# Turning the next quarter of x behind the product blocks of two tiles, in place of at the quarter's change

## The reference, cut to what matters

```
h = rmsnorm(x, norm_w)                       # x is 2048 x 1024
u = h @ w_in                                 # here the columns of RWKV
mixed = u + (prev_token(u) - u) * mu         # r, k, v and the two low-rank inputs
decay = exp(-exp(w(tanh(wl)))), a = sigmoid(al @ a_up + a0)
S_t = S_{t-1} (diag(w_t) - kk_t^T (a_t kk_t)) + v_t^T k_t ;  y_t = S_t r_t
out = (groupnorm(y) + bonus) * silu(g)
```

## Time and profile before

| | |
|---|---|
| median of 3 runs | 3938.05 us (3936.14 to 3941.47) |
| the profiled execution's own time | 3943.03 us |
| its span, first to last instruction | 3941.3 us |
| PE busy in the span | 3507.1 us (89%) |
| DVE, ACT, POOL busy | 1894.0, 1273.3, 798.4 us |
| stream stage, from the span's start to its last instruction | 1066 us |

### The profile page before, as it was taken

How to read it: one execution, slowest core, us unless ns; L and a number is a source line. 1 busy time by engine, 2 the same in 40 slices (tenths; PEclk the granted TensorE clock), 3 DMA queues, 4 the chain that set the end, 5 groups by cost and what they waited for, 6 DMA issues and landing times. The chain is left out here.

```text
span 3941.3 us, 72212 instructions
## 1 busy us (share of the span) xinstructions
PE 3507.1 (89%) x30237; PEld 2860.4 (73%) x30237; DVE 1894.0 (48%) x2915; ACT 1273.3 (32%) x1970; POOL 798.4 (20%) x592
## 2 busy tenths in 40 slices
PE   6989989899698898797999998960699999999998
PEld 4777878778534344586888886850699999999997
DVE  4455656556522133366212225669455555555553
ACT  3343534444221222233000002330344444444442
POOL 3333434333167093000000000011010010110100
PEclk9999999999899899898999999985899999999999
DMA  4121121111132131343110105440466666666663
GB/s 129 45 79 45 43 82 43 55 47 29 60 121 79 44 107 33 128 136 94 27 53 27 53 11 183 155 138 13 158 199 218 203 214 204 201 218 207 208 207 86
DMA packets 357752, 431.44 MB, mean 109 GB/s; under 512 B 14788, under 2 KB 301684, under 8 KB 356004
## 3 DMA queue, kind: packets, MB, share of 16 engines
q1 hardware_dynamic: 348328, 394.82, 31.1%
q0 software_dynamic: 9216, 33.56, 3.6%
HBM read 361.04 MB, written 67.13 MB: 109 GB/s over the span
## 5 line engine op out<-in xcount | busy, mean ns | idle before, releaser
L1983 PE MATMUL bank<-ex_x_hi,ex_w_lo 128*128 128x256 f32 x2048 | 580.3, 283 | 1.5 <-DVE ex_x_lo L2152 1.5
L1984 PE MATMUL bank<-ex_x_lo,ex_w_hi 128*128 128x256 f32 x2048 | 580.2, 283 | 0.0
L1985 PE MATMUL bank<-ex_x_hi,ex_w_hi 128*128 128x256 f32 x2048 | 580.1, 283 | 0.0
L1979 DVE TENSOR_TENSOR ex_w_lo<-ex_w_loaded,ex_w_hi 128x2048 fp32r<-128x2048 f32 x186 | 420.7, 2290 | 235.6 <-ACT ex_w_hi L1975 235.6
L1975 ACT ACTIVATE ex_w_hi<-ex_w_loaded 128x2048 fp32r<-128x2048 f32 x192 | 359.8, 1905 | 199.6 <-PE bank L1985 183.9
L1983 PEld LDWEIGHTS bank<-ex_x_hi,ex_w_lo 128*128 128x128 f32 x2048 | 393.9, 192 | 2.5 <-issue 1.9
L1984 PEld LDWEIGHTS bank<-ex_x_lo,ex_w_hi 128*128 128x128 f32 x2048 | 393.8, 192 | 0.6
L1985 PEld LDWEIGHTS bank<-ex_x_hi,ex_w_hi 128*128 128x128 f32 x2048 | 393.8, 192 | 0.0
L1227 PE MATMUL bank<-hidden_hT,gl_w_block 128*128 128x512 f32 x768 | 335.1, 599 | 1.4 <-ACT gl_ada_acc L1341 1.4
L1778 PE MATMUL bank<-sc_x_hi,sc_w_lo 128*128 128x512 f32 x768 | 300.4, 391 | 21.8 <-DVE sc_hT_lo L1814 16.3
L1779 PE MATMUL bank<-sc_hT_lo,sc_w_hi 128*128 128x512 f32 x768 | 299.5, 390 | 0.0
(11 more groups left out here) (334 smaller groups left out, 7083.6 us busy)
## 6 DMA issues: line engine op xcount, KB each, us to landing
ex_w_loaded<-in_wg SPq DMA_DIRECT2D x64, 1024.0 KB, 5.2
ex_w_loaded<-in_wu SPq DMA_DIRECT2D x64, 1024.0 KB, 6.5
ex_w_loaded<-in_wd SPq DMA_DIRECT2D x64, 1024.0 KB, 5.2
rw_w_loaded<-in_w_in SPq DMA_DIRECT2D x68, 512.0 KB, 3.9
gl_ada_tile<-in_ada_w SPq DMA_DIRECT2D x48, 512.0 KB, 3.9
sc_w_loaded<-in_sc_w_in SPq DMA_DIRECT2D x24, 512.0 KB, 6.9
rw_x_tile<-in_x SPq DMA_DIRECT2D x16, 512.0 KB, 4.9
hT_dram<-rw_h_staged SPq DMA_DIRECT2D x32, 256.0 KB, 2.8
```

The costliest lines, as they stand in the source:

```text
L1979: engine.tensor_tensor(w_lo[c % SPLIT][:], raw[:, c % LOADED, :], w_hi[c % SPLIT][:].bitcast(F32), ALU.subtract).then_inc(s["lo"], 1)
L1983: nc.tensor.matmul(psum, ll, rh, start=first, stop=False)
L1984: nc.tensor.matmul(psum, lh, rl, start=False, stop=False)
L1985: return nc.tensor.matmul(psum, lh, rh, start=False, stop=last)
```

## The change

The staging buffer is gone. A result of turning is written back into the half of the x tile that it was read from (`staged`), and rounding, subtraction and the store read it there. Turning goes by halves of four transposes, numbered x = 0 to 7 in a quarter, one ring job each. In the last two tiles of a quarter (i % 4 is 2 or 3) one half is turned after the PE work of parts 2 and 4 of the first half and of parts 1 and 3 of the second (`turned_in`), and DVE and SP take it one part later (`staged_in`). The rounding and subtraction of all eight stand at the quarter's change: those of the first four blocks of rows at the end of the last tile, the others in part 0 of the next one (`split_in`). The product k of that tile waits for the two portions apart. The first tile of a quarter then has its jobs in the order k, lr, w, a, r, v, g, with r, v and g in halves as in other tiles. Loading, squares and scaling of x are in the first and second tile of the quarter instead of the last. Before the first tile all eight halves are turned and split at once.

```
+        staged = lambda x: xt[:, x // 2 % 4, x % 2 * 512:x % 2 * 512 + 512].rearrange("p (k t) -> p k t", t=P)
...
-                return ({4: ("k",)}, {0: ("lr",), 1: ("r",), 3: ("v",), 4: ("g",)})[half].get(part, ())
+                return ({1: ("k",), 2: ("lr",)}, {0: ("r",), 2: ("v",), 4: ("g",)})[half].get(part, ())
...
+        def turned_in(i, half, part):
+
+            n = {(0, 2): 0, (0, 4): 1, (1, 1): 2, (1, 3): 3}.get((half, part))
+            if n is None or i >= NT - HP or i % HP < 2:
+                return ()
+            return (8 * (i // HP + 1) + 4 * (i % HP - 2) + n,)
+
+        def staged_in(i, half, part):
+
+            return turned_in(i, half, part - 1) if part else turned_in(i - 1 + half, 1 - half, 4)
+
+        def split_in(i, half, part):
+
+            if (half, part) == (1, 4) and i < NT - HP and i % HP == HP - 1:
+                return [8 * (i // HP + 1) + 2 * n for n in range(4)]
+            if (half, part) == (0, 0) and HP <= i < NT and i % HP == 0:
+                return [8 * (i // HP) + 2 * n + 1 for n in range(4)]
+            return []
...
                     for part in parts:
+                        if name == "k" and i % HP == 0:
+                            pe.wait_ge(s["h_lo_p"], 4 * q + 2 * part + 2)
+                            pe.wait_ge(s["h_lo_v"], 4 * q + 2 * part + 2)
...
+                    if i < NT and half == 0 and i % HP == 0:
+                        if part < 2:
+                            product(i, ("k", "lr")[part], (0, 1))
+                        elif part == 2:
                             decay_and_a(i)
+                        else:
+                            product(i, "r", (part - 3,))
...
+                    for x in turned_in(i, half, part):
+                        turn_x(x)
                     if half == 1 and part == 4:
                         if i < NT:
                             bonus_sum(i)
                         if 0 <= i - 3 < NT:
                             turn_y(i - 3)
-                        if i % HP == HP - 1 and i < NT - 1:
-                            turn_x(4 * (i // HP + 1))
...
+                def load_x(q):
+
+                    sp.wait_ge(s["h_lo_p"], 4 * q)
+                    sp.wait_ge(s["h_lo_v"], 4 * q)
+                    for n in range(4):
+                        sp.wait_ge(hs_out[n], 32 * q)
+                        sp.dma_start(xt[:, n, :], x[0, (4 * q + n) * P:(4 * q + n + 1) * P, :]).then_inc(x_in[n], 16)
...
+                        for e in staged_in(i, half, part):
+                            keep_h(e)
+                        if half == 0 and part == 1 and i % HP == 0 and i < NT - HP:
+                            load_x(i // HP + 1)
                         for name in finished(i, half, part):
...
                     if i < NT and i % HP == 0:
+                        if (half, part) == (0, 2):
+                            keep_lora(i // HP)
+                            keys(i)
+                        if (half, part) == (0, 3):
+                            decay_and_a(i)
                         if (half, part) == (1, 0):
                             exponents(i)
...
-                    if i % HP == HP - 1 and i < NT - 1:
+                    if i % HP == 1 and i < NT - HP:
                         q = i // HP + 1
```

More of the change, by code:

```diff
@@ L442, in _ @@
                 pe.wait_ge(s["small"], 16 * SMALL)
-                turn_x(0)
+                for x in range(8):
+                    turn_x(x)
                 for g in slots:
@@ L535, in _ @@
                     load(n)
+                for e in range(8):
+                    keep_h(e)
                 load(3)
@@ L539, in _ @@
                     for part in range(5):
[L540 to L545, removed]
+                        if half == 0 and part == 0 and 0 <= i - 4 < NT:
+                            store(i - 4)
+                        for e in staged_in(i, half, part):
+                            keep_h(e)
+                        if half == 0 and part == 1 and i % HP == 0 and i < NT - HP:
+                            load_x(i // HP + 1)
                         for name in finished(i, half, part):
@@ L548, in _ @@
                             load(n + 4)
-                        if half == 0 and part == 1 and 0 <= i - 4 < NT:
-                            store(i - 4)
                 sp.wait_ge(s["stored"], 16 * NT)
                 for n in range(4):
-                    sp.wait_ge(hs_out[n], 16 * 8)
+                    sp.wait_ge(hs_out[n], 32 * Q)
             @block.scalar
@@ L660, in pump @@
                 def pump(i, half, part):
-                    for t in x_of(i, half, part):
-                        keep_hi(2 * t)
-                        keep_hi(2 * t + 1)
+                    for e in split_in(i, half, part) if half == 0 else []:
+                        keep_hi(e)
                     for name in finished(i, half, part):
@@ L726, in _ @@
                     split_hi(n)
+                for e in (0, 2, 4, 6, 1, 3, 5, 7):
+                    keep_hi(e)
                 act.wait_ge(s["derived"], 1)
@@ L935, in pump @@
                             mix_raw(i, "r", r)
+                    if i < NT:
                         if (half, part) == (1, 1):
@@ L944, in pump @@
                             form_of_r(i)
-                    if i % HP == HP - 1 and i < NT - 1 and (half, part) == (1, 0):
+                    for e in staged_in(i, half, part):
+                        keep_h(e)
+                    for e in split_in(i, half, part)[1::2] if half else []:
+                        keep_lo(e)
+                    if i % HP == 1 and i < NT - HP and (half, part) == (1, 0):
                         scale_x(i // HP + 1)
@@ L1016, in _ @@
                     nc.vector.tensor_scalar(xt[:, t, :], xt[:, t, :], xst[:, 3, t:t + 1], None, ALU.mult).then_inc(s["scaled"], 1)
+                for e in range(8):
+                    keep_h(e)
+                for e in (2, 6, 3, 7):
+                    keep_lo(e)
                 for g in slots:
@@ L1103, in _ @@
                     split_lo(n)
+                for e in (0, 4, 1, 5):
+                    keep_lo(e)
                 for g in slots:
@@ L1111, in _ @@
                     for part in range(5):
-                        for t in x_of(i, half, part):
-                            keep_lo(2 * t)
-                        if i < NT and (half, part) == ((1, 2) if i % HP == 0 else (0, 2)):
+                        for e in split_in(i, half, part)[0::2] if half == 0 else []:
+                            keep_lo(e)
+                        if i < NT and (half, part) == ((0, 4) if i % HP == 0 else (0, 2)):
                             before_step(i)
@@ L1121, in _ @@
                             split_lo(windex[(i, name)] + 3)
+                        for e in split_in(i, half, part)[0::2] if half else []:
+                            keep_lo(e)
         meet(nc, s)
```

148 lines of the change are left out of this document (55 added, 93 removed).

## The result

The changed kernel takes 3990.99 us in the median of 4 runs (3989.33 to 3993.06), where the kernel before took 3937.1 beside it (3934.55 to 3941.47). The ratio is 1.0136 [1.0121, 1.0151]: 54 us slower. The direction was the one forecast, the size was not: 3959 was named, with 3980 as the upper end.

The account below looks back on a forecast made before the run. PE was taken to bound the stream stage. Terms -48.3 + 64.7 + 3.0 - 1 + 3 made +21 us on the profiled 3943.03, 3964, less 5.0 to the median: 3959 us, range 3934 to 3980.

Parts of the forecast that it names:

- gain at the three quarter changes: Stretches around each quarter's change, without half turnings, take 96.6 us each instead of 338.1 in all: 48.3 us gained, bounds 36 and 64.
- turnings in six tiles: Tiles 2, 3, 6, 7, 10, 11 each get 2.2 us of PE transposes of x: 13.2 us cost.
- ring waits: With x between jobs, blocks wait for later readers in the two-bank ring: 8.8 us a tile, 51.5 in six, bounds 40 and 62.
- scaling: Scaling x, now in a quarter's second tile, stands before a copy of the next slot: 1.0 us three times, bounds 0 and 4.
- start: At the start k could begin 3.6 us earlier, but the low-rank chain stands open: -1 us, bounds -4 and +5.
- clock: PE's clock falls after waits of 3.6 us at two of six places: 3 us, bounds 0 and 22.
- wait 1.9: At a quarter's change, block k waits 1.9 us for its first portion of low parts.
- wait 2.3: At a quarter's change, block k waits 2.3 us for the second portion, behind ACT and DVE's and POOL's subtractions.
- I take 1.8: At a quarter's change, w waits 1.8 us, between 0 and 3.5, for the low-rank inputs.
- New wait 3.6, 2.6, 1.6, 1.0: Per turning tile: r waits for k's mix, v for r's, g for v's, bonus for ACT's reading of g, in that order.
- The clock falls at every longer ring wait: Rival, chance 0.13: 11 waits of 2.6 and 3.6 us each followed by 12 matmuls at 1.2 GHz, +17 over forecast, 3976 us.
- wait for weights: Rival, chance 0.09: x loads ahead of g's weights delay ACT up to 8 us at tiles 0, 4, 8; 3975 to 3983.

Follow-up runs that it names:

- experiment 1: The changed kernel, but the block after a turned half takes that half's bank and DVE reads the half at once: 3910.05 us, ratio 0.9936 to the kernel before.
- experiment 3: The kernel before, turning unchanged, with the change's waits of r, v, g and bonus added in tiles 2, 3, 6, 7, 10, 11: 4008.73 us, ratio 1.0178.
- experiment 6: The kernel before with only block g's wait for the mix of v added in the six tiles: 3948.17 us, ratio 1.0025.
- experiments 7 and 8: Experiment 1's kernel plus the change's waits by hand, 3987.82 us (7); or plus 16, 11 and 7 extra matmuls ahead of r, v, g, 3965.45 us (8).
- its repeat: Experiment 1's kernel measured once more, unchanged: 3914.36 us, ratio 0.9942 to the kernel before.
- experiments 4 and 8: 16, 11 and 7 extra matmuls ahead of r, v, g in six tiles: on the kernel before 3986.51 us (4), on experiment 1's 3965.45 us (8).

## Why the prediction was wrong

Its mechanism was right, and so was every term but one. In us, forecast and measured (profiled execution):

| term | forecast | measured |
|---|---|---|
| gain at the three quarter changes | -48.3 | -46.2 |
| turnings in six tiles | +13.2 | +10.6 |
| ring waits | +51.5 | +49.1 |
| scaling | +3.0 | +1.9 |
| start | -1 | -1.8 |
| clock | +3 | +37 |
| stream stage | +21 | +50.7 |

- **What goes.** "96.6 a change": the new tile's first half took 41.36, of which 1.57 is clock (twelve matmuls of k after its second wait in 4.6 us in place of 3.0), the second 29.2; with an ordinary 28.26 before them that is 97.3, and 338.1 less three times this is 46.2. Inside it "wait 1.9" for the first portion was 2.1, "wait 2.3" for the second 2.5, "I take 1.8" for w was 1.6. Right. The profile names DVE's bonus reading for the first of them, not the low part: k is also bound by the ring there, at nearly the same time (at tile 8 POOL's subtraction ends at 540.16 us, DVE's bonus reading at 540.42), which the prediction did not have.
- **The turnings.** 1.8 a tile by experiment 1, where 2.2 was forecast. Right.
- **The ring.** "New wait 3.6, 2.6, 1.6, 1.0" were 3.54, 2.40, 1.48 and 0.99, and r's in tile 2 was 2.2 (1.4 less, as said). The earlier trace rows had both ends of each wait in them, and experiment 3 shows the same waits without the transposes. Right.
- **The rest.** No wait for weights arose: ACT waits for them once, 5.3 us at the program's start, as before. The start's 1.8 is within what the start differs between runs (experiment 6). Scaling is tile 6's 0.6 over tile 7 in experiment 1, three times.
- **The step that failed** is the clock in "The rest": "waits of 3.6 will do so at some of the six places. I take two, 3 us, bounds 0 and 22". It is the remainder of the stage here, 50.7 less 13.6 for the other terms. 29 of the 37 can be pointed at: in the changed kernel the twelve matmuls after the r, v and g waits took 4.4 to 5.5 us in 17 of 18 places, where 3.0 is the price at 2.4 GHz; another 4.7 are block k after its second wait, and the last 3 are a remainder that is not pinned down. From 3959 to 3991 it is 32 us: 34.1 more for the clock, 4.8 less for the other terms, 1.7 less behind the stage, 4.0 because the prediction took 5.0 off from the profiled execution to the median and it is 1.0 in the change, and 0.4 of rounding.

The rival "The clock falls at every longer ring wait" was what happened, and for the waits that it counts its price was right: 11 waits at 17 + 3 = 20 us, where r's and v's 11 falls cost 19.7 (1.4 to 1.6 each where the block reached 2.4 GHz before its end, 2.5 in the three r blocks that ran wholly at 1.2 GHz). Its sum of 3976 was too low because it left out the rest: g's waits of 1.5, six falls and 9.6 us, which experiment 6 shows to be enough in four of six places, and the 4.7 of block k. Its argument against itself, that the 1.27 us waits of ordinary tiles leave the share at 1.00, was true and no evidence for waits longer than those.

The prediction also misread the trace of before, which already held both sides. It says that the clock "fell in the two first halves after waits of 1.7 and 2.1". Here are the turnings of tiles 4 and 8, each with waits of 2.1, 2.3 and 0.8 us after the first of 1.7, and then block k's first twelve matmuls after the waits of 5.6 at tiles 4, 8 and 12:

```profile
236.09:261.14 25.05, 19.79 (x414) 17.71 (x414) 15.82 (x31) 7.83 (x18) 5.96 (x6) 0.86 0.47 135
491.39:513.55 22.16, 16.90 (x414) 14.91 (x414) 15.63 (x31) 7.78 (x18) 5.97 (x6) 1.00 0.52 148
266.69:271.63 4.94, 4.94 (x13) 3.93 (x14) 0.00 (x0) 0.08 (x1) 3.40 (x6) 0.58 0.74 223
519.11:524.12 5.01, 5.01 (x13) 3.97 (x14) 0.00 (x0) 0.08 (x1) 3.40 (x6) 0.57 0.73 220
775.65:780.41 4.76, 4.75 (x13) 3.81 (x14) 0.00 (x0) 0.09 (x1) 3.41 (x6) 0.60 0.45 121
```

After the waits of some 2 us the clock fell at tile 4 and stayed at 1.00 at tile 8; after those of 5.6 it was down three times of three. So the clock can fall after waits of 2 us and need not. A fall at every new wait over 1.3 us, 18 times 1.5 to 2.5, is 27 to 45 us and a time of 3983 to 4001; the upper end of the range had to go there. (Its lower end has a slip: 64 for 48.3 and 40 for 51.5 make 3932, not 3934.) The Trainium skill, "TensorE: Matmul & The Clock Gate", section "A second HAM failure mode: psum-queue depth-cycling", says that short idles between groups of matmuls, in a kernel that cycles through PSUM banks, make the clock swing between half and full and cost throughput; experiments 7 and 8 agree with it, 25 us beside 51 of waiting and none in the slots that were filled with work.

It stays open why a fall comes at some places and not at others. The change has it in 17 of 18, experiment 7 with equal waits in 12 of 18 (in tiles 2 and 3 its r waits of 2.3 and 3.6 and its v waits of 2.5 were followed by full clock), experiment 3 in 13. In the change block k of a new quarter took 3.0 us after its first wait of 2.1 in all three quarters, and 4.6 after its second of 2.5. Experiment 1 and its repeat are one and the same kernel and differ in this too. Block k of tile 4, its two halves in the one and then in the other:

```profile
243.31:247.79 4.48, 4.48 (x12) 3.24 (x12) 4.41 (x5) 0.64 (x2) 4.28 (x4) 0.65 0.16 59
248.89:251.89 3.00, 3.00 (x14) 2.21 (x16) 0.00 (x0) 0.00 (x0) 0.00 (x0) 1.00 0.64 191
242.52:245.54 3.02, 3.01 (x12) 2.17 (x12) 2.99 (x4) 0.64 (x2) 3.02 (x4) 1.00 0.23 85
248.08:252.66 4.58, 4.58 (x14) 3.22 (x16) 0.00 (x0) 0.00 (x0) 0.00 (x0) 0.63 0.77 265
```

The first wait was 2.1 us in both. So where a fall comes is in part the execution's and not the kernel's. No run separates what distinguishes the places. So the 37 us have a cause that was shown, and a number of falls that one can bound and not derive.

## What to carry to other kernels

In a ring of two banks, ask of every job that is put in between two others whom the next one now waits for; give the next job the bank of the short-lived one, and have that one read at once (3910 us with both, 4008 with the bank and the late reading). Price a new wait on the matrix engine at its length and at the block after it at half the clock, whenever it is longer than the waits that the trace shows to be harmless. Where waits are exact to a tenth of a microsecond and the clock is taken by feel, the clock is where the range must be wide.

## What the runs showed of the hardware

- A wait of 1.5 us on PE, between the 64x64 matmuls of the recurrence and a block of 128x512 ones, was followed by 1.2 GHz in 6 of 6 places in the change and in 4 of 6 when it was the only one (experiment 6). The wait of 1.27 us in every ordinary tile never was.
- In the change, twelve matmuls took 4.5 to 5.5 us after waits of 3.5, 4.4 to 4.6 after waits of 1.5 to 2.4 (but for one place), and 3.0 at full clock.
- Two profiled executions of one kernel had the fall at different places: at tile 4 in block k's first half in the one, in its second half in the other (experiment 1 and its repeat).
- The same slots filled with matmuls in place of waiting stayed at 1.00 (experiments 4 and 8).
